# A two-layer decoder step: the samples' last stage takes two page groups together

## The reference, cut to what matters

```python
s_s = jnp.einsum('btgrd,btgkjd->btgrkj', q, ks) * sc      # selected pages (32 of 128 tokens a sample)
p_s = masked_softmax(s_s.reshape(...), mask_s.reshape(...))
o_s = jnp.einsum('btgrm,btgmd->btgrd', p_s, vs.reshape(...))
p_w = masked_softmax(jnp.einsum('btgrd,bsgd->btgrs', q, kw) * sc, mask_w)   # window of 512 tokens
o_w = jnp.einsum('btgrs,bsgd->btgrd', p_w, vw.astype(jnp.float32))
```

## Time and profile before

| | |
|---|---|
| median of 3 runs | 1221.73 us (1216.88 to 1222.3) |
| the profiled execution | 1219.12 us, its span 1217.5 us |
| TensorE (PE) busy | 1160.9 us, 95% of the span |
| VectorE, ScalarE, GpSimd busy | 487.7, 424.7, 206.2 us |
| granted TensorE clock, mean | 0.976 of 2.4 GHz |
| moved by DMA | 238.76 MB, mean 196 GB/s |

### The profile page before, as it was taken

The page is one execution under the profiler, slowest core; times in us unless marked ns, Lnnn a source line. Parts: engine busy times, 40 slices in busy tenths (PEclk is TensorE's granted clock), DMA queues, the critical chain, the costliest instruction groups (busy, mean ns, idle before and its releaser), DMA issues.

```text
span 1217.5 us, 25231 instructions
## 1 busy us (share of the span) xinstructions
PE 1160.9 (95%) x9077; PEld 740.8 (61%) x9077; DVE 487.7 (40%) x1500; ACT 424.7 (35%) x1079; POOL 206.2 (17%) x347
## 2 busy tenths in 40 slices
PE   3899999999989999999999999999999979999995
PEld 1677774666767757567777656655555434445552
DVE  1544032345441430202300666656667623433345
ACT  3322113233221321010110465666666434444442
POOL 0000000000000011112211222222223344433400
PEclk8899999999999999999989999999999999999998
DMA  9654435303036112225035756776676499999972
GB/s 378 288 208 173 159 134 203 139 1 139 1 155 214 69 69 74 74 74 194 8 107 181 274 200 227 272 273 225 241 259 219 139 357 357 356 356 353 355 260 79
DMA packets 97015, 238.76 MB, mean 196 GB/s; under 512 B 12794, under 2 KB 50812, under 8 KB 92540
## 3 DMA queue, kind: packets, MB, share of 16 engines
q1 hardware_dynamic: 73468, 164.95, 38.0%
q0 software_dynamic: 23424, 72.21, 17.0%
HBM read 227.57 MB, written 17.05 MB: 201 GB/s over the span
## 4 chain that ended last, share of the span: by engine, by line
PE 88%; DMA 6%; DVE 3%; SPq 1%; issue 1%; ACT 1%; DVEq 1%; ACTq 0%
PE ps L412 28%; PE ps L423 7%; PE ps L1252 5%; PE ps L2292 5%; PE ps L1892 5%; PE ps L2441 4%; PE ps L1756 4%; DMA wring<-in_weights 3%; PE ps L1796 3%; PE ps L1779 3%; PE ps L2332 3%; PE ps L2313 3%; DMA wring<-in_win_kv 1%; PE ps L1577 1%; PE ps L1928 1%; PE ps L394 1%
## 5 line engine op out<-in xcount | busy, mean ns | idle before, releaser
L412 PE MATMUL ps<-arena,wring 128*128 128x288 f32 x1408 | 364.0, 416 | 2.2 <-DMA wring<-in_weights 2.2
L412 PEld LDWEIGHTS ps<-arena,wring 128*128 128x128 f32 x1408 | 267.4, 193 | 85.9 <-issue 14.2
L1736 POOL DMA_DIRECT2D arena<-in_cmp_pages x128 | 71.4, 558 | 237.7 <-PE ps L1899 135.7
L423 PE MATMUL ps<-wring,arena 128*128 128x512 f32 x192 | 90.1, 604 | 0.0
L1827 DVE CUSTOM_DVE_ANT_0 wring<-ps,wring 128x128 f32<-128x128 f32 (+3 forms) x128 | 57.6, 488 | 72.0 <-PE ps L1756 71.7
L2378 DVE CUSTOM_DVE_ANT_1 arena<-ps,small 128x512 f32<-128x512 f32 x64 | 44.3, 693 | 97.1 <-PE ps L2292 97.1
L1819 ACT ACTIVATE wring<-ps 128x128 f32<-128x128 f32 (+3 forms) x128 | 49.1, 435 | 84.2 <-PE ps L1779 84.1
L1805 ACT ACTIVATE wring<-wring,arena 128x128 f32<-128x128 f32 (+3 forms) x128 | 70.6, 559 | 4.0 <-DVE arena L1827 4.0
L2354 ACT ACTIVATE arena<-arena 128x512 f32<-128x512 f32 (+1 forms) x88 | 56.9, 648 | 40.6 <-DVE arena L2394 40.6
L2365 ACT ACTIVATE arena<-ps 128x512 f32<-128x512 f32 x72 | 43.0, 597 | 80.7 <-PE ps L2313 80.7
L1892 PE MATMUL ps<-arena 128*32 128x256 f32 x1024 | 68.2, 382 | 0.0
(11 more groups left out here) (391 smaller groups left out, 1622.7 us busy)
## 6 DMA issues: line engine op xcount, KB each, us to landing
wring<-in_weights SPq DMA_DIRECT2D x27, 2048.0 KB, 10.5
arena<-in_cmp_pages SPq DMA_DIRECT2D x128, 256.0 KB, 4.8
arena<-in_cmp_pages POOLq DMA_DIRECT2D x128, 256.0 KB, 5.8
wring<-in_kv_pages SPq DMA_DIRECT2D x56, 256.0 KB, 7.7
wring<-in_kv_pages POOLq DMA_DIRECT2D x56, 256.0 KB, 7.0
arena<-in_kv_pages POOLq DMA_DIRECT2D x56, 256.0 KB, 7.1
arena<-in_kv_pages SPq DMA_DIRECT2D x56, 256.0 KB, 11.4
out_win_k_out<-in_win_kv SPq DMA_DIRECT2D x8, 512.0 KB, 12.1
```

Source lines behind the costliest of these rows:

```text
L412: last = pe.matmul(out[:, 0:HT], w[:, k, ct * P:ct * P + P], moving[k][:, half * HT:half * HT + HT], start=(k == 0), stop=(k == KT - 1))
L423: last = pe.matmul(main, tokens, w[:, k, :], start=(k == 0), stop=(k == KT - 1))
L1736: eng.dma_start(cring[page_slot(q)][:, 2 * half + j, :], v["cmp_pages"][bass.ds(ids[2 * d + j], 1)] .rearrange("o p c -> (o p) c")).then_i ...
```

## The change

It does these things:

- In every pass TensorE takes two groups together: two groups' transposes, then two groups' values, then two groups of the next sample's scores. Before, it took one of each in turn. ScalarE runs two exponentials ahead and not one, and PTr has four slots, in another place. The norm's sum of the last pass moves from `at == 5` to `at == 6`.
- The first seven scores of sample 0 are taken two a step (steps 63 to 66; the seventh alone in 66).
- Sample 1's pages are loaded apart, in the order keys 0 to 5, values 0 to 3, keys 6 and 7, values 4 to 7, by the new `load_apart`. Scores of sample 1 then wait for keys alone and its values are waited for where they are used.
- The homes are dealt out anew. Sample 1's first four groups of keys go to ring[5], ring[6], ring[0], ring[1]; the first two are free in unit 7's first steps, the next two in steps 70 and 71. Its values 0 to 3 now wait for the prompt's last values.

The diff, cut to its core:

```diff
-        k_homes = ring[0:4] + [vv0, vv1, c0, s0]
-        v_homes = [ring[5], ring[6], ring[7], ring[9], LAST_KEYS, z0, z1, c1] + [ring[8], ring[10], ring[11], ring[4], s1, s2, HEAD_KEYS, s3]
+        k_homes = [ring[5], ring[6], ring[0], ring[1]] + [vv0, vv1, c0, s0]
+        v_homes = [ring[8], ring[7], ring[2], ring[3], LAST_KEYS, z0, z1, c1] + [ring[9], ring[10], ring[4], ring[11], s1, s2, HEAD_KEYS, s3]
-        PTr = ph_[:, 0:3 * TP].rearrange("p (s n) -> p s n", s=3)
+        PTr = arena[:, kcT_at - 4 * TP:kcT_at].rearrange("p (s n) -> p s n", s=4)
...
+            elif at == 0:
+                eng.wait_ge(pe_a, PE3["t", U - SU, 0])
+            elif at == 1:
+                eng.wait_ge(pe_a, PE3["pv", U - SU])
             elif at < 4:
-                eng.wait_ge(pe_a, PE3["t", tile_step[at - 4], 1])
+                eng.wait_ge(pe_a, PE3["t", tile_step[at - 6], 1])
...
+        def load_apart(eng, half, part):
+
+            if part == 0:
+                for pair in range(3):
+                    load_keys(eng, half, 1, pair)
+            elif part == 1:
+                for pair in range(2):
+                    load_values(eng, half, 1, pair)
+            elif part == 2:
+                load_keys(eng, half, 1, 3)
+            else:
+                for pair in range(2, 4):
+                    load_values(eng, half, 1, pair)
...
+        def inside_of(i):
+            return [x for x in range(INSIDE) if U - SU + x // 2 == i]
...
-            if n * NJ + at >= 3:
-                act.wait_ge(valued, n * NJ + at - 2 if at >= 3 else n * NJ)
+            if n * NJ + at >= 4:
+                act.wait_ge(valued, n * NJ + at - 3 if at >= 4 else n * NJ)
...
-                if 0 <= i - (U - SU) < INSIDE:
-                    pe_scores(pe, 0, i - (U - SU))
+                for x in inside_of(i):
+                    pe_scores(pe, 0, x)
...
-                for at in range(NJ + 1):
-                    if at <= LAST:
+                for at in range(0, NJ + 2, 2):
+                    if at < NJ:
                         pe_turn(pe, n, at)
-                    if at >= 1:
+                        pe_turn(pe, n, at + 1)
+                    if at >= 2:
+                        pe_values(pe, n, at - 2)
                         pe_values(pe, n, at - 1)
-                    if n < NB - 1 and at >= 2:
-                        pe_scores(pe, n + 1, at - 2)
-                    if n == NB - 1 and at == 5:
+                        if n < NB - 1:
+                            pe_scores(pe, n + 1, at - 2)
+                            pe_scores(pe, n + 1, at - 1)
+                    if n == NB - 1 and at == 6:
...
             for n in range(NB):
                 act_exp(act, n, 0)
+                act_exp(act, n, 1)
                 for at in range(NJ):
-                    if at < LAST:
-                        act_exp(act, n, at + 1)
+                    if at + 2 < NJ:
+                        act_exp(act, n, at + 2)
                     act_turned(act, n, at)
```

More of the change, by code:

```diff
@@ L2160, in build @@
                 v_total[h, n, i] = v_count[h][values_sem(n, i)]
-                if n and i < NG:
+                if n > 1 and i < NG:
                     continue
@@ L2204, in wait_values_home @@
                 eng.wait_ge(pe_a, PE3["s", 4 * SU - 1])
-            elif at < 4:
-                eng.wait_ge(pe_a, PE3["t", tile_step[at - 4], 1])
-                if at == 2:
+            elif at == 10:
+                eng.wait_ge(scored, NG + 1)
+            elif at <= 4 or 8 <= at <= 11:
+                eng.wait_ge(pe_a, PE3["pv", U - 1])
+                if at == 1:
                     eng.wait_ge(dve_c, DC_["sel", NB - 1])
-            elif at == 4 or 8 <= at < 11:
-                eng.wait_ge(pe_a, PE3["pv", U - 1])
-                if at == 10:
+                if at == 11:
                     eng.wait_ge(dve_a, DV3["m", U - 1, 1])
-            elif at == 11:
-                eng.wait_ge(scored, NG + 1)
             elif at == 14:
@@ L2273, in pe_scores @@
                 for h in range(2):
-                    if n:
+                    if n > 1:
                         pe.wait_ge(v_in[h][values_sem(n, i)], v_total[h, n, i])
@@ L2318, in pe_values @@
             pe.wait_ge(copied, n * NJ + at + 1)
-            if n == 0 and j < NG:
+            if n <= 1 and j < NG:
                 for h in range(2):
-                    pe.wait_ge(v_in[h][values_sem(0, j)], v_total[h, 0, j])
+                    pe.wait_ge(v_in[h][values_sem(n, j)], v_total[h, n, j])
             if j == NG:
@@ L2325, in pe_values @@
                 pe.wait_ge(*((combined, n) if n else (dve_a, DV3["o", 7])))
-            pt = PTr[:, at % 3, :]
+            pt = PTr[:, at % 4, :]
             def add(x, m, at_row, values, start, stop):
@@ L2359, in act_turned @@
             act.wait_ge(turned, n * NJ + at + 1)
-            if n * NJ + at >= 3:
-                act.wait_ge(valued, n * NJ + at - 2 if at >= 3 else n * NJ)
+            if n * NJ + at >= 4:
+                act.wait_ge(valued, n * NJ + at - 3 if at >= 4 else n * NJ)
             if JS[at] == NG + 1:
-                last = act.activation(PTr[0:NS, at % 3, 0:2 * P], ps[0:NS, 4 + at % 2, 0:2 * P], ACT.Copy)
+                last = act.activation(PTr[0:NS, at % 4, 0:2 * P], ps[0:NS, 4 + at % 2, 0:2 * P], ACT.Copy)
             else:
-                last = act.activation(PTr[:, at % 3, :], ps[:, 4 + at % 2, :], ACT.Copy)
+                last = act.activation(PTr[:, at % 4, :], ps[:, 4 + at % 2, :], ACT.Copy)
             last.then_inc(copied, 1)
@@ L2487, in sp_third @@
                 for pair in range(NG // 2):
-                    load_kv(sp, 0, n, pair)
+                    if n == 1:
+                        load_apart(sp, 0, pair)
+                    else:
+                        load_kv(sp, 0, n, pair)
                 load_window_keys(sp, n)
@@ L2516, in pool_third @@
                 for pair in range(NG // 2):
-                    load_kv(pool, 1, n, pair)
+                    if n == 1:
+                        load_apart(pool, 1, pair)
+                    else:
+                        load_kv(pool, 1, n, pair)
                 load_window_values(pool, n)
@@ L2561, in pe_third @@
                         pe.matmul(ps[:, 0, :], ones, f_acc, start=True, stop=True).then_inc(f_summed, 1)
-                if n < NB - 1:
-                    pe_scores(pe, n + 1, LAST)
             pe_out_turn(pe, NB - 1)
@@ L2637, in dve_third @@
                     prompt_cmp_probs(dve, 1)
-                if 0 <= i - (U - SU) < INSIDE:
-                    dve_scores(dve, 0, i - (U - SU))
+                for x in inside_of(i):
+                    dve_scores(dve, 0, x)
                 if U <= i < U + NJ - INSIDE:
```

## The result

The changed kernel takes **1229.09 us** (median of 15 runs, 1223.31 to 1233.06) against 1220.11 us for the kernel before (15 runs, 1216.76 to 1225.54): a ratio of **1.0064**, 95% interval [1.0048, 1.008]. It is slower by 0.64%, 7.8 us (the two medians are 9.0 us apart), and outside the forecast's range of 1205 to 1227 us. The profiled execution took 1230.58 us, with a span of 1228.9 us.

The account below looks back on a forecast made before the run. Page transfers at about 357 GB/s were taken to bound the passes. Terms -4.7 + 2.4 - 0.6 - 0.7 + 0.5 (clock after new waits) = -3.1 us, from 1221.7 to 1218.6 us; range 1205 to 1227 us.

Parts of the forecast that it names:

- The bound: Passes over the samples: page transfers at about 357 GB/s, 9.95 MB a pass, hold them at 27.9 us, not TensorE.
- The first rival: Passes: TensorE is the bound after all, so they shrink by 16 us and pass 0 by up to 12; 1194 us, chance 0.15.
- the second: Passes: the transfers have a little left, 366 GB/s, 0.7 us less a pass; about 1213.7 us, chance 0.17.
- The third: Output tile 7 and last pass: waiting for the last pages leaves TensorE at 1.2 GHz; about 1228 us, chance 0.15.
- -4.7, the slack: End of the stage: merging gains only the 4.7 us between sample 7's window keys landing and TensorE scoring them.
- The price of a boundary: TensorE's passes: each of 13 merged boundaries between kinds of work saves 0.21 us, 2.7 us a pass.
- -5.4 us: Pairs: the 4.7 us of slack at sample 7's window keys plus 0.7 us in the last pass.
- what GpSimd has fetched ahead for sample 2 by then is less by as much: Pass 0: it may end up to 6 us earlier, but the bytes are the same; costed at nothing.
- +2.4, loads apart: Sample 1's loads: 128 KB pieces at 301 GB/s cost 3.9 us, earlier homes give back 1.5; net +2.4 us.
- Early scores: Steps 63 to 66: seven scores two a step merge three boundaries, -0.6 us.
- The last pass: Fourth slot, exponentials two ahead: where ScalarE sets the pace, the third exponential runs under the output tile, -0.7 us.
- The start gap, -1.5: 966 to 970 us, DMA share 0.65 and 0.60: homes free earlier for four groups of keys recover 1.5 us.

Follow-up runs that it names:

- the coupled kernel with pairs: Only the passes paired, GpSimd starting two groups' pages once SyncE's half from two pairs back landed (samples 2 to 7), against the kernel before: 1218.82 us, ratio 0.9986.
- the pairs alone: Kernel before with only the passes changed: two groups together, four slots, exponentials two ahead; old loads, homes and early scores: 1227.41 us, ratio 1.0047.
- the coupled kernel before: Kernel before, with only GpSimd made to wait for SyncE's landed half from two pairs back (samples 2 to 7): 1215.90 us, ratio 0.9964.
- half pages: Kernel with only the passes paired, where samples 3 to 7 load and use half of their pages' columns: one run, 1210.21 us.
- the loads apart without any reading: Kernel before with new homes and sample 1's loads apart, its page numbers fixed in the program: 1218.38 us, ratio 0.9993; with the readings 1.0043.

## Why the prediction was wrong

**The bound was read rightly.** Merged passes are held by the transfers: from 1034 to 1166 us the coupled kernel with pairs moves 354 and 355 GB/s and the kernel before 355 and 356, each at a share of 1.05 or 1.06, and the passes of the coupled kernel with pairs take 28.0 to 28.6 us although TensorE could do them in 26.8. This agrees with the 358 GB/s of the Trainium skill (DMA: Bandwidth & Descriptors, Bandwidth). What sets the rate for these loads is not shown; weights came at 436 GB/s in the same kernel. The first rival (TensorE the bound) and the second (366 GB/s) are out. The third, slower by TensorE's clock, had the sign but neither place nor mechanism: tile 7 starts late, and the last pass is no longer than before. Clock is lost, but in pass 1 (0.86) and behind the fetch waits (0.50 from 1124 to 1126 us, behind that of 1.82 us).

**The step "-4.7, the slack" failed in how it was to be had.** The price of a boundary was 0.15 us, not 0.21, and two waits for ScalarE, 0.9 us a pass, came with the new order; TensorE's pass is 26.8 us, not 25.2. That alone would still have let the slack be used. What failed is the condition "as long as the transfers keep their time". Instead of -5.4 us (the slack and the last pass) the pairs alone measured +0.47%, 5.7 us, and sample 7's window keys land at 1175.1 us in them, 7.1 us later than before. In their trace GpSimd's queue takes the homes at once, and SyncE's half of the same groups, without which no score can start, comes 10 us later; TensorE then stands and frees no homes, and later the DMA engines run low: a share of 0.74 at 1136 us in the pairs alone, 0.58 at 1056 us in the changed kernel. I had set down that "what GpSimd has fetched ahead for sample 2 by then is less by as much" and costed it at nothing, with full DMA engines for cover. Full engines are no cover when they bring the wrong half. Without the lead the changed kernel is 5.3 us faster and the pairs alone 8.6 us (1227.41 to 1218.82), but the kernel before 5.2 us too (1221.09 to 1215.90): the lead was there already and cost time there too. How much of it merging adds, and what else makes coupled pairs 0.22% slower than the coupled kernel before, stays open; the fetch waits are one candidate (with half pages a pass with 2.21 us of them took 30.7 us and not 26.8), and no kernel takes them away.

**The step "+2.4, loads apart" had the wrong cause.** I took the lower rate from the size of the pieces and wrote of the page numbers that "nothing waits for that while about 10 us of transfers are in flight". In this stretch a transfer lands 3 to 4 us behind its issue, and 1.37 us of reading before 2.3 us of issuing leave the DMA engines short. From 976 to 1004 us they move 278 GB/s in place of 349 to 366, window keys 1 land late, and half of the readings alone cost 5.6 us, where +2.4 was forecast for the whole; the loads apart without any reading measured 0.9993, no loss. This is the surest of the causes: three pairs of kernels show it.

**The terms that held.** Early scores: -0.6 forecast, nothing measured. The last pass: -0.7 forecast, 0.4 us shorter in the profiled executions. The start gap, -1.5, was not closed: from 966 to 970 us the share is 0.44, against 0.65 and 0.60. The whole sum of the changes, once both causes are out, is 1218.5 us: the forecast's number, 1218.6, but with two repairs in it that the change did not have, one of which is worth as much without the change. That the numbers meet is luck.

## What to carry to other kernels

When two queues bring halves of one tile and share full DMA engines, the one that runs ahead does so at the other's cost; tie the leader to what the follower has landed (0.31 to 0.61% in five kernels here). Homes that come free late can do this by accident, as in the kernel before, and a change elsewhere takes it away. Put a repair into the kernel before as well: only then can its gain be told from the cost of the change. Before splitting loads, count what each issue carries with it on its engine, register reads too, and look at how much is in flight in that very stretch.

## What the hardware showed that was not expected

When groups are taken in pairs, TensorE stops at some places of its program, multiples of 256 records apart, for 0.3 to 3.1 us, and is slower for some us behind the long stops: in the changed kernel pass 4 has waits of 0.4 and 1.8 us, eight score products behind them take 2.95 us in place of 1.95, the granted clock from 1124 to 1126 us is 0.50, and the pass takes 31.2 us. It waits for the next 16 KB of its own program. It came with DMA engines at a share of 0.77 as well as with full ones, and where only transposes stand in pairs (1.52 us) as well. The kernel before, at 27.9 us a pass, passes the same counts only 1.4 us or more behind the landing of the packet, in all but two cases over 2 us, and shows no such wait. Why the packets come when they come is open.
